# A 2 MB weight transfer of a fused decoder layer, split into three parts of uneven rows

## The reference

```python
h = rmsnorm(x, mix_norm_g)
u = h @ w_in                                  # (256, 3600)
x = x + concat(mlstm(u), moba_attention(u)) @ w_out
t = rmsnorm(x, ffn_norm_g)
gates = softmax over the top 4 of 32 of (t @ w_router + b_router)
for e in range(32):
    hu = t @ w_gate_up[e] + b_gate_up[e]      # w_gate_up[e]: (1024, 2048), 8 MB
    act = clamped_swiglu(hu)
    y += gates[:, e:e+1] * (act @ w_down[e] + b_down[e])   # w_down[e]: (1024, 1024), 4 MB
x = x + y
x = x + sigmoid(rmsnorm(x, ple_norm_g) @ w_ple_gate) * (p @ w_ple_proj)
```

## Time and profile before

| | |
|---|---|
| median of 3 runs | 1115.68 us |
| the profiled execution, own time | 1118.58 us |
| its span (first to last instruction) | 1116.8 us |
| mean granted TensorE clock | 0.996 |
| TensorE matmul busy | 1073.1 us (96%) |
| VectorE, ScalarE, GpSimd busy | 23%, 13%, 1% |
| HBM read | 430.04 MB, 386 GB/s over the span |
| chain that ended last | PE 64%, DMA 33% |

### The profile page before, as it was taken

How to read it: one execution, slowest core, us unless ns; L and a number is a source line. 1 busy time by engine, 2 the same in 40 slices (tenths; PEclk the granted TensorE clock), 3 DMA queues, 4 the chain that set the end, 5 groups by cost and what they waited for, 6 DMA issues and landing times.

```text
span 1116.8 us, 12032 instructions
## 1 busy us (share of the span) xinstructions
PE 1073.1 (96%) x5140; PEld 445.3 (40%) x5140; DVE 257.4 (23%) x533; ACT 144.4 (13%) x283; POOL 16.4 (1%) x40
## 2 busy tenths in 40 slices
PE   8999999999999999999999999898989999989898
PEld 4476564434343434343434233333333344423234
DVE  2364333131211111221212111121211021212122
ACT  3233432010000000000000000000000100000012
POOL 1000200000000000000000000000000000000000
PEclk9999999999999999999999999999999999999999
DMA  9941589999999999999999999999999999999971
GB/s 348 343 179 76 217 329 376 429 427 426 428 428 427 428 428 427 426 428 429 427 427 428 427 428 427 428 428 427 427 427 427 428 425 428 429 427 427 429 310 38
DMA packets 42398, 431.89 MB, mean 387 GB/s; under 512 B 6008, under 2 KB 6528, under 8 KB 17128
## 3 DMA queue, kind: packets, MB, share of 16 engines
q1 hardware_dynamic: 42272, 431.07, 92.4%
q10 hardware_dynamic: 72, 0.04, 0.0%
HBM read 430.04 MB, written 1.06 MB: 386 GB/s over the span
## 4 chain that ended last, share of the span: by engine, by line
PE 64%; DMA 33%; DVE 1%; ACT 1%; issue 0%; ACTq 0%; DVEq 0%
DMA ring<-in_w_gate_up 30%; PE hu L1051 22%; PE po L1081 14%; PE aux L1006 5%; PE hu L692 5%; DMA ring<-in_w_down 4%; PE hu L698 3%; PE aux L1014 2%; PE hu L1043 2%; PE hu L708 2%; PE aux L1244 1%; PE po L1058 1%; PE hu L1081 1%; PE po L1244 1%; PE hu L1244 1%
## 5 line engine op out<-in xcount | busy, mean ns | idle before, releaser
L1051 PE MATMUL hu<-ring,num_xg 128*64 128x512 f32 x1920 | 433.4, 598 | 26.8 <-DMA ring<-in_w_gate_up 26.6
L1051 PEld LDWEIGHTS hu<-ring,num_xg 128*64 128x64 f32 x1920 | 131.7, 137 | 309.1 <-issue 256.4
L1081 PE MATMUL po<-ring,arena 128*64 128x512 f32 x976 | 217.8, 596 | 5.9 <-DMA ring<-in_w_down 5.9
L1081 PEld LDWEIGHTS po<-ring,arena 128*64 128x64 f32 x976 | 67.2, 137 | 152.8 <-issue 136.0
L1594 DVE TENSOR_SCALAR arena<-hu 128x512 f32<-128x512 f32 x31 | 21.4, 692 | 433.4 <-PE hu L1051 433.4
L1570 DVE TENSOR_TENSOR arena<-arena,aux 128x512 f32<-128x512 f32 x58 | 37.3, 684 | 134.2 <-PE aux L1014 122.4
L692 PE MATMUL hu<-ring 128*128 128x512 f32 x144 | 63.8, 596 | 0.0
L1006 PEld LDWEIGHTS aux<-num_xg,big 128*128 128x128 f32 x512 | 58.4, 192 | 13.0 <-issue 13.0
L1006 PE MATMUL aux<-num_xg,big 128*128 128x128 f32 x512 | 61.4, 278 | 0.0
L1903 ACT ACTIVATE hu<-arena 128x512 f32<-128x512 f32 x31 | 18.6, 601 | 252.8 <-DVE arena L1594 252.8
L1583 DVE TENSOR_SCALAR arena<-iota_s,posm,gates 128x128 f32<-128x128 f32 x64 | 17.9, 343 | 118.2 <-PE po L1081 115.3
(11 more groups left out here) (275 smaller groups left out, 597.1 us busy)
## 6 DMA issues: line engine op xcount, KB each, us to landing
ring<-in_w_gate_up SPq DMA_DIRECT2D x126, 2048.0 KB, 38.1
ring<-in_w_down SPq DMA_DIRECT2D x61, 2048.0 KB, 38.9
ring<-in_w_in SPq DMA_DIRECT2D x6, 2048.0 KB, 17.0
ring<-in_w_out SPq DMA_DIRECT2D x2, 2048.0 KB, 8.8
ring<-in_w_gate_up SPq DMA_DIRECT2D x4, 1024.0 KB, 6.2
ring<-in_w_ple_gate SPq DMA_DIRECT2D x2, 2048.0 KB, 35.1
ring<-in_w_down SPq DMA_DIRECT2D x3, 1024.0 KB, 6.8
ring<-in_w_in SPq DMA_DIRECT2D x2, 1024.0 KB, 8.6
```

Source lines behind the costliest of these rows:

```text
L1051: last = mm(hu[n * SLOTS:(n + 1) * SLOTS, 2 * e + b, :], rows_of[:, k, e * SLOTS:(e + 1) * SLOTS], w[:, o:o + NB], start=first, stop=(k == ...
L1081: last = mm(bank[n * SLOTS:(n + 1) * SLOTS, :], actT[:, f, h * SLOTS:(h + 1) * SLOTS], w[:, o:o + NB], start=(h == 0 and f == 0), stop=(h ...
```

## The change

The first up transfer of the last pair, position 181, is issued as three transfers where it was one. The first takes columns 0 to 1535 of rows 0 to 123, the second the same columns of rows 124 to 127, the third columns 1536 to 4095 of all 128 rows. The first two add to semaphores of their own, the third to the slot's `ring_full`. In `up_chunk` TensorE waits for the two new semaphores and then, as before, for `ring_full`.

```diff
+    UNEVEN_AT = AT.index((PAIRS - 1, 0, 0, 0))
+    UNEVEN_ROWS, UNEVEN_COLS = 124, 1536
...
+        most_rows_in = sem("most_rows_in")
+        last_rows_in = sem("last_rows_in")
...
                 if m in HALVED:
                     sp.dma_start(dst[:, 0:2 * D], src[:, 0:2 * D]).then_inc(half_loaded, 16)
+                elif m == UNEVEN_AT:
+                    r, c = UNEVEN_ROWS, UNEVEN_COLS
+                    sp.dma_start(dst[0:r, 0:c], src[0:r, 0:c]).then_inc(most_rows_in, 16)
+                    sp.dma_start(dst[r:P, 0:c], src[r:P, 0:c]).then_inc(last_rows_in, 16)
+                    sp.dma_start(dst[:, c:4 * D], src[:, c:4 * D]).then_inc(full, 16)
                 else:
                     sp.dma_start(dst, src).then_inc(full, 16)
...
                         if m in HALVED:
                             wait_half(pe, ps, m)
+                        if m == UNEVEN_AT:
+                            pe.wait_ge(most_rows_in, ps * 16 + 16)
+                            pe.wait_ge(last_rows_in, ps * 16 + 16)
                         wait_position(pe, ps, m)
```

## The result

The changed kernel takes 1124.37 us (median of 4 runs, 1123.2 to 1125.24); the kernel before, in the same comparison, 1116.25 us (4 runs, 1114.54 to 1117.2). The ratio is 1.0069, interval 1.0055 to 1.0083: slower by about 7.7 us (6.1 to 9.3). The profiled execution took 1124.03 us, close to its median, while the one of before (1118.58) stood 2.3 us above the median of its four runs. So the two traces differ by 5.5 us where the medians differ by 8. In the comparison with 27 executions of the kernel before, further down, two of these were slow (1848.73 and 2426.78 us), and the ratios leave them out.

A forecast was written before the change was run, and what follows sets the result against it. The DMA stream at 428 GB/s was taken to bound the kernel, TensorE having caught up. Terms 0 + 0 + 0 + 4.6 us (12.9 - 8.3) on the 1115.7 median gave 1120.3 us, range 1113.6 to 1125.5.

The forecast's parts named there:

- Rival A: Four engines at position 181 are early and disturb nobody: 0.8 to 1.8 us faster, 1113.9 to 1114.9 us; chance 0.28.
- Rival C: The 124 rows spread over all sixteen engines: at most 0.9 us change, 1114.8 to 1116.6 us; chance 0.14.
- term 6: Four engines at the stream's end lead the last by 6.3 to 10.3 us, middle 8.3, leaving 4.6 us slower.
- term 5: SBUF writes of the four engines, sharing ways in, cost double: four 12.9 us later, twelve net nothing.
- Terms 1 to 3: At position 181, two more SyncE issues, more and smaller packets, and two more TensorE waits: each costs nothing.
- Term 4: 124 rows go to four engines, 31 each: four 5.5 us later, twelve 1.83 us sooner.
- the tail's end: Sign at the stream's end: the DMA share's tail ends some 5 us later; earlier than 1087 would refute the forecast.
- long flat foot at 4/16: Sign at the stream's end: the tail of the DMA share has a long flat foot at 0.25.
- the DMA share did not fall below 1: Sign expected in the stream: the DMA share falls below 1 for some stretch while only a few engines lag.
- Rival B: The four engines at position 181 are of the late half: slower, 1118 to 1129 us; chance 0.13.

The follow-up runs named there:

- the second profile: The changed kernel run once more, unchanged, against the kernel before: 1124.26 us against 1116.81, ratio 1.0069.
- the second profile of before: The kernel before run once more, unchanged, for a second profile: 1117.0 us, against 1118.58 in its first profiled execution.
- The two runs with writes to HBM: Changed kernel with its first two parts sent to HBM scratch: 1.0005 of before; kernel before plus those two copies to HBM: 1.0028.
- The kernel with every fourth row: Against before, columns 0 to 3071 load only 32 rows, in eight transfers of four rows, every fourth row each: 1113.4 us, ratio 0.9968.
- the part of 1024 columns to HBM: Changed kernel with 1024 instead of 1536 columns in the first two parts, written to HBM scratch: 1116.52 us, 1.0001 of the kernel before.
- the pair of kernels above: Two kernels loading the same 32 rows in four-row transfers, every fourth row or side by side: 1113.4 and 1114.85 us, 0.9968 and 0.9984 of before.

## Why the prediction was right or wrong

**The side and most of the chain of reasons held, the size did not.** The forecast was +4.6 us, measured were +7.7; 1120.3 lies 4.1 us under the 1124.37. Rivals A and C fall: there is a dip and a wait of 4.67 us at the first up chunk. The term of the sum that was mis-sized is the lead (term 6); term 5 has a part that is wrong in kind. The two errors pull opposite ways: term 5 was 1.4 us too large, the lead 3.7 us, and the first hides some of the second.

**Terms 1 to 3 (issues, packets, waits: nothing)** held: three parts cut by columns gave 1.0004. The two issues took far longer than the 0.33 us that they were priced at, yet inside the cover that was named. SyncE's timeline of after:

```profile
982.49 0.32 SPq L503 DMA_DIRECT2D ring<-in_w_gate_up  x1
982.85 5.64 SPq L504 DMA_DIRECT2D ring<-in_w_gate_up  x1
988.53 2.38 SPq L505 DMA_DIRECT2D ring<-in_w_gate_up  x1
```

The long one goes with the dealing to four engines: in the second profile it takes 5.08 us, with 112 or 64 rows the same issue takes 0.43 and 0.59. From the end of the last at 990.91 to TensorE's start at 1028.43 there are still 37.5 us.

**Term 4 (124 rows on four engines)** held. Small packets are 6016 where the second profile of before has 6008: one transfer's 16 became 24 = 4 + 4 + 16, as foretold. All packets are 136 more, 128 data packets and these 8. Rival C's spreading is thereby out; with 112 rows, where every part uses sixteen engines, it is 32 more. The rule of the Trainium skill (DMA: Bandwidth & Descriptors, section "Why a DMA increments its semaphore by 16 and not by 1"), quoted with the term, is borne out in the number of engines; which ones they are no view names.

**Term 5 (where the four write)** is near for the four and wrong for the twelve. It had a pair share a way, the four 12.9 us later, and the twelve "net nothing" (lose 1.83 us, gain 1.83). The windows show another thing: not some engines but the stream as a whole falls to 248 of 427 GB/s, 5.0 to 5.6 us that every engine loses. Balanced engines lose as much (112 rows: +6.0 us; 64 rows: +6.2). So it is not a doubled price on the astray rows but about 6 us for everybody per 768 KB cut by rows, whoever carries them. In that account the four are 6.0 + 5.5 = 11.5 us later, which 12.9 came near to, by luck, as the doubling behind it is not what happened, and the twelve 6.0 - 1.83 = 4.2 us later, where the prediction had 0. As the four set the end in both accounts, the sum forgave it; with 112 rows, where no engine carries more, the doubled price would have given each engine 8 x 0.23 = 1.8 us for what cost 6.

The Trainium skill (DMA: Bandwidth & Descriptors, section "Back-pressure in remote DMA") says for transfers between cores that a full way into SBUF backs up to its source and to other engines on the same path. No transfer here is between cores, but the rows show what such a backing-up would give: engines at full share and 58% of the rate.

**Term 6 (the lead)** is the step that failed in size: "if they are of the early half, they lead by 6.3 to 10.3 us; middle 8.3". The two runs with writes to HBM give 4.9 and 4.2 us. The prediction read the ramp of rows 5 at the middle of its early half, as if the four were one; what counts is the least early of them. A lead of 4.6 us, the mean of the two, is 1083.2 in rows 5 and 1081.4 in the second profile of before, whose stream ends at about 1086: the share is 0.47 and 0.52 there. So the least early of the four would stand about midway among the sixteen, and "of the early half" was too much for all four. With 4.6 in its place, the prediction's own sum is 12.9 - 4.6 = 8.3 us; with term 5 as the runs have it, 11.5 - 4.6 = 6.9. Measured: 7.7 (6.1 to 9.3).

The corrected terms (they were fitted to runs that had been made, and are no forecast), scaled by the columns, against the other sizes: with 512 columns the twelve set the end, 2.0 - 0.6 = +1.4 us (measured +1.0, -0.1 to +2.0); with 3072 the four, 12 + 11 - 4.6 = +18.4 (measured +22.0, 20.1 to 23.9). The largest is short by 3.6 us. Its windows say where most of that is: the stream itself loses 14.1 us and not 12, which gives 14.1 + 11 - 4.6 = 20.5, inside the interval. The dips of 2.3, 5.6 (6.7) and 14.1 us for 512, 1536 and 3072 columns are near proportion to the bytes within one way of dealing. Across ways of dealing that is not shown.

**What would show it.** The small packets, the wait, the dip and the tail's end about 5 us later came as written. The "long flat foot at 4/16" did not: the share at the end is 0.31, 0.18, 0.06 in 1088 to 1091, a ramp. The four are not last by a distance, since most of what they lost all engines lost. And the DMA share did not fall below 1 in the dip: engines that are held up count as busy. **Rival A's** gain, 1.8 us, fails on both legs: rows disturb all, and the lead is under 7.3. **Rival B** had no lead at all, and that is excluded by the two runs with writes to HBM.

**Is there a version that beats the kernel before?** None was found. Cut by columns nothing changes; small enough to cost little (512 columns), the part costs more than it gives back. The kernel with every fourth row leaves out weights and is no candidate. Engines did come relieved at their price there, so a split that gives early engines more rows, and only rows of their own, might gain; the rows of the late engines, though, are by the map above theirs alone, and moving them is what costs. That was not tried.

**What stays open.** Where the way narrows that all engines share (no view names engines or ways); what sets its price, as it is not simply the bytes astray: if each engine gets rows that lie side by side, then by the map above half of the 64 + 64 rows and only about an eighth of the 112 + 16 rows go where they belong, and both cost 6 us (no run shows how 64 rows are dealt); and why the part of 1024 columns to HBM shows no gain.

## What to carry to other kernels

A transfer on 128 partitions runs at full rate, most likely because each DMA engine writes rows of its own: the pair of kernels above speaks for it. A cut by rows (here 124 + 4, and also the balanced 112 + 16 and 64 + 64) slows the whole stream while it lasts: here 768 KB cost about 6 us on top of the 1.8 that they normally take. So cut a large transfer by columns, not by rows, and to find such a fault look at GB/s beside the DMA share: share 1.00 at 248 GB/s is engines that are held up, here by where they write.

## What the runs showed of the hardware that was not expected

- Four engines copying 768 KB from HBM to HBM beside the stream don't slow it: 429 GB/s in 1008 to 1020 us. The same bytes written into SBUF rows of other engines bring it to 248.
- 64 + 64 rows, sixteen engines with eight rows each as always, cost as much as 112 + 16: +6.2 us. The Trainium skill (SBUF — State Buffer, section "Door 1: The DMA port swizzle") has 64 adjacent partitions reach half of 16 ports. By that alone 768 KB at half of 428 GB/s would lose an estimated 1.8 us; the run lost over three times as much.
- An issue on SyncE can take 5.64 us, for a transfer of four rows behind one of 124, both on four engines; in rows 9 the longest took 4.0, and behind 112 rows on sixteen engines it is 0.43.
- The granted clock fell to 0.50 (the 1.2 GHz level) in 1026 to 1028 us, after TensorE had stood idle since 1023.8, and the first chunk behind it took 5.71 us for 3.65. These 2.1 us cost nothing: TensorE waits for the stream again at 1058.66.
- The least early of the four engines that a 124-row transfer uses reaches the end of the stream 4 to 5 us ahead of the last one. What makes engines drift apart over a millisecond no run here shows.
